# Mixer rows of x at a stride of 2304 bytes, 64 bytes behind the weight ring's residue, and all Mixer tiles over 528 columns

## The reference

```python
h = x @ w_in                    # 528 x 1024 times 1024 x 8192
b_c, c_c, h_c, q, k, v, g_conv, g_attn = split(h)
y_conv = b_c * causal_dwconv(c_c * h_c, conv_w_mix)
o = stick_breaking_attention(q, k, v)         # 16 heads of 64
merged = sigmoid(g_conv + b[0]) * (y_conv @ w_proj_conv) \
       + sigmoid(g_attn + b[1]) * (o @ w_proj_attn)
mix = merged @ w_out
# h + rms_norm(mix), then the feed-forward with its own convolution; the last 512 rows are the output
```

## Time and profile before

| what | value |
| --- | --- |
| median of 3 runs | 1918.76 us (1917.21 to 1919.23) |
| the profiled execution | 1915.86 us, of which 1914.1 us are the span |
| TensorE busy | 1900.1 us, 12180 matmuls |
| VectorE, ScalarE, GpSimd busy | 1041.9, 764.5, 66.8 us |
| the rows' DMA, mean | 88 GB/s |

### The profile page before, as it was taken

The page is one execution under the profiler, slowest core; times in us unless marked ns, Lnnn a source line. Parts: engine busy times, 40 slices in busy tenths (PEclk is TensorE's granted clock), DMA queues, the critical chain, the costliest instruction groups (busy, mean ns, idle before and its releaser), DMA issues.

```text
span 1914.1 us, 31604 instructions
## 1 busy us (share of the span) xinstructions
PE 1900.1 (99%) x12180; PEld 1694.7 (89%) x12180; DVE 1041.9 (54%) x1635; ACT 764.5 (40%) x1270; POOL 66.8 (3%) x119
## 2 busy tenths in 40 slices
PE   8999999999999999999999999999999999999998
PEld 8888888899888888888999999999999799999887
DVE  5777767445253455532646555565666464444334
ACT  5545444333233333322435554555642242333222
POOL 3000000000010000000100000000000010000000
PEclk9999999999999999999999999999999999999999
DMA  6322222232323333323232222222122233333331
GB/s 173 85 67 77 69 64 78 77 88 78 120 89 110 99 88 90 92 92 121 78 89 78 78 68 78 77 78 78 57 78 89 88 94 98 94 90 96 109 100 55
DMA packets 244260, 167.81 MB, mean 88 GB/s; under 512 B 5293, under 2 KB 231701, under 8 KB 244166
## 3 DMA queue, kind: packets, MB, share of 16 engines
q1 hardware_dynamic: 242368, 160.98, 28.4%
q10 hardware_dynamic: 1286, 4.23, 0.7%
q0 software_dynamic: 512, 1.24, 0.2%
HBM read 164.33 MB, written 2.10 MB: 87 GB/s over the span
## 4 chain that ended last, share of the span: by engine, by line
PE 92%; DVE 4%; ACT 2%; issue 1%; DMA 0%; POOL 0%; DVEq 0%; POOLq 0%; SPq 0%; ACTq 0%
PE pj L1860 9%; PE pj L1861 9%; PE pj L1862 9%; PE pj L1320 7%; PE pj L1322 7%; PE pj L1321 7%; PE zz L1320 2%; PE zz L1322 2%; PE zz L1321 2%; PE oa L1383 2%; PE tr L1383 2%; PE tr L1385 2%; PE oa L1385 2%; PE tr L1384 2%; PE oa L1384 2%; PE pj L1383 2%
## 5 line engine op out<-in xcount | busy, mean ns | idle before, releaser
L2188 DVE TENSOR_TENSOR w_lo<-raw,w_hi 128x1024 fp32r<-128x1024 f32 x299 | 364.9, 1222 | 248.4 <-ACT w_hi L681 244.6
L681 ACT ACTIVATE w_hi<-raw 128x1024 fp32r<-128x1024 f32 x299 | 314.3, 1054 | 209.5 <-PE tr L1385 140.5
L1860 PE MATMUL pj<-xx,w_hi 128*128 128x256 f32 (+2 forms) x1280 | 364.2, 285 | 0.5 <-DVE s_kl L2787 0.5
L1861 PE MATMUL pj<-xx,w_hi 128*128 128x256 f32 (+2 forms) x1280 | 360.7, 282 | 0.0
L1862 PE MATMUL pj<-xx,w_lo 128*128 128x256 f32 (+2 forms) x1280 | 360.3, 282 | 0.0
L1320 PE MATMUL pj<-xx,w_hi 128*128 128x512 f32 x632 | 252.3, 399 | 0.4 <-DVE qs L2332 0.4
L1322 PE MATMUL pj<-xx,w_lo 128*128 128x512 f32 x632 | 246.5, 390 | 0.0
L1321 PE MATMUL pj<-xx,w_hi 128*128 128x512 f32 x632 | 246.2, 390 | 0.0
L1860 PEld LDWEIGHTS pj<-xx,w_hi 128*128 128x128 f32 x1280 | 240.9, 188 | 1.9 <-issue 0.7
L1861 PEld LDWEIGHTS pj<-xx,w_hi 128*128 128x128 f32 x1280 | 241.0, 188 | 0.7
L1862 PEld LDWEIGHTS pj<-xx,w_lo 128*128 128x128 f32 x1280 | 241.1, 188 | 0.0
(11 more groups left out here) (624 smaller groups left out, 3731.8 us busy)
## 6 DMA issues: line engine op xcount, KB each, us to landing
raw<-in_l_w_in_dram SPq DMA_DIRECT2D x113, 512.0 KB, 4.1
raw<-in_w_in_dram SPq DMA_DIRECT2D x64, 512.0 KB, 4.1
raw<-in_w_up_gate_dram SPq DMA_DIRECT2D x44, 512.0 KB, 3.9
raw<-in_l_w_out_dram SPq DMA_DIRECT2D x32, 512.0 KB, 3.5
raw<-in_w_down_dram SPq DMA_DIRECT2D x22, 512.0 KB, 3.4
raw<-in_w_proj_conv_dram SPq DMA_DIRECT2D x8, 512.0 KB, 4.2
raw<-in_w_proj_attn_dram SPq DMA_DIRECT2D x8, 512.0 KB, 4.1
raw<-in_w_out_dram SPq DMA_DIRECT2D x8, 512.0 KB, 3.5
```

Of the source, the lines that this page charges most:

```text
L681: act.activation(w_hi[:, slot], raw[:, slot], ACT.Copy).then_inc(hi_done, 1)
L1860: pe.matmul(dst, w_hi[:, slot, k, :], hi[:, k, tok], start=(k == 0), stop=False)
L1861: pe.matmul(dst, w_hi[:, slot, k, :], lo[:, k, tok], start=False, stop=False)
L2188: dve.tensor_tensor(w_lo[:, slot], raw[:, slot], w_hi[:, slot].bitcast(F32), ALU.subtract).then_inc(lo_done, 1)
```

## The change

The Mixer's rows are set 576 tokens (2304 bytes) apart, beginning 64 bytes into the region of x (`XOFF` = 16 elements). Since 2304 is 9 x 256, each row then starts at the ring's residue plus 64, modulo 256. All eight tiles of a round are computed over all 528 tokens, `FULL`, 256 and 272; of q, b, c, h and the gates only the last 516 are taken from PSUM, through `P_HALF` (0 to 244 and 244 to 516 of the destination) and `P_COLS` (columns 12 to 256 of the first bank, 0 to 272 of the second). `c_hi` and `c_lo` become the first 516 elements of the same rows. The region of x grows by 3072 bytes, and the region of constants shrinks by 576: `ones_r`, `rs_hi`, `rs_lo` and `spread_rows`, which nothing called, go. To make room, small buffers of the meta tokens (`s_km`, `s_qm`, `s_zm`, `s_aTm`) move to the 48 free elements at the rows' ends, `ub`, `m_sel0` move behind the rows of the first model, `gained` of the last two junctions moves to B and `yf` to the start of A. No wait is added or removed.

```diff
@@ -155,7 +155,7 @@
...
-        const = region(4960 + 4 * P + 64 + 4 * NM)
+        const = region(4960 + 4 * NM)
@@ -165,9 +165,6 @@
...
-        ones_r = sb(const, "ones_r", [P, P], F32R)
-        rs_hi = sb(const, "rs_hi", [P, NT], F32R)
-        rs_lo = sb(const, "rs_lo", [P, NT], F32R)
@@ -203,18 +200,26 @@
...
-        X = region(2 * KD * TF * 4)
-        XA = [X[0], X[0], X[0] + 2 * KD * 576 * 4]
-        xx = sb(XA, "xx", [P, 2 * KD * 576], F32R)
+        XROW, XOFF = 576, 16
+        X = region(2 * KD * XROW * 4)
+        xx = sb([X[0], X[0], X[2] + XOFF * 4], "xx", [P, 2 * KD * XROW + XOFF], F32R)
+        X_TAIL = 2 * KD * TF * 4
...
-        x_hi, x_lo = x_view(0, TF), x_view(KD * TF, TF)
-        x3_hi, x3_lo = x_view(0, 576), x_view(KD * 576, 576)
-        X3 = 576 - T
+        x_hi, x_lo = x_view(XOFF, XROW), x_view(XOFF + KD * XROW, XROW)
+        c_hi, c_lo = x_hi[:, :, 0:TA], x_lo[:, :, 0:TA]
+        gap = sb([X[0], X[0], X[2] + XOFF * 4], "gap", [P, 2 * KD * XROW + XOFF])
+        gaps = gap[:, XOFF:XOFF + 2 * KD * XROW].rearrange("p (k t) -> p k t", k=2 * KD)
+        s_km = gaps[:, 0:KD, TF:TF + NM]
+        s_qm = gaps[:, 0:KD, TF + NM:TF + NM + MA]
+        s_zm = gaps[:, KD:KD + 2, TF:TF + NM]
+        s_aTm = gaps[:, KD + 2:KD + 6, TF:TF + 2 * NM]
+        x3_hi, x3_lo = x_view(0, XROW), x_view(KD * XROW, XROW)
+        X3 = XROW - T
@@ -222,10 +227,10 @@
...
-        def junction(q, reg, reg_gained=None):
+        def junction(q, reg):
...
-            gained[q] = sb(reg_gained or reg, f"gained{q}", [P, D])
+            gained[q] = sb(reg, f"gained{q}", [P, D])
@@ -244,8 +249,7 @@
...
-        X3_BYTES = XA[1] - X[2]
-        junction(3, again(B, KF * T * 4 + X3_BYTES - (A[2] - A[0])), again(W, (W[2] - W[0] - D * 4) // 32 * 32))
+        junction(3, again(B, KF * T * 4 - (A[2] - A[0])))
@@ -314,7 +318,7 @@
...
-        m_sel0 = sb(again(W, 227520 - 187488), "m_sel0", [GROWS, P], F32R)
+        m_sel0 = sb(again(X, X_TAIL), "m_sel0", [GROWS, P], F32R)
@@ -333,7 +337,7 @@
...
-        ub = sb(w_, "ub", [P, T])
+        ub = sb(again(X, X_TAIL + 4 * P), "ub", [P, T])
@@ -349,9 +353,6 @@
...
-        X_ = again(X)
-        c_hi = sb(X_, "c_hi", [P, KD, TA], F32R)
-        c_lo = sb(X_, "c_lo", [P, KD, TA], F32R)
@@ -362,25 +363,19 @@
...
+        assert w_[1] <= W[0] + AT_W
...
-        s_qm = sb(w_, "s_qm", [P, NP, MA])
-        s_km = sb(w_, "s_km", [P, NP, NM])
...
-        assert w_[1] <= W[0] + AT_W
-        w_ = again(W, AT_W)
...
+        s_me = sb([w_[0], w_[1], w_[2]], "s_me", [MA, HS * NM])
...
-        s_zm = sb(w_, "s_zm", [P, 2, NM])
...
-        s_aTm = sb(w_, "s_aTm", [P, P])
-        s_me = sb(w_, "s_me", [MA, HS * NM])
-        yf = sb([A[0], A[0] + X3_BYTES, B[2]], "yf", [P, KF, T])
+        yf = sb([A[0], A[0], B[2]], "yf", [P, KF, T])
@@ -394,7 +389,6 @@
...
-        assert w_[1] <= W[2] - D * 4 - 32
@@ -459,6 +453,8 @@
...
+        P_HALF = [slice(0, T // 2 - A0), slice(T // 2 - A0, TA)]
+        P_COLS = [slice(A0, T // 2), slice(0, TF - T // 2)]
@@ -1083,7 +1079,7 @@
...
-                    ins, done = act.activation(s_qh[:, par, HALF[hf]], src[:, 0:HN[hf]], ACT.Copy, scale=QD ** -0.5), "q"
+                    ins, done = act.activation(s_qh[:, par, P_HALF[hf]], src[:, P_COLS[hf]], ACT.Copy, scale=QD ** -0.5), "q"
@@ -1096,15 +1092,15 @@
...
-                    ins, done = act.activation(cb[:, HALF[hf]], src[:, 0:HN[hf]], ACT.Copy), "b"
+                    ins, done = act.activation(cb[:, P_HALF[hf]], src[:, P_COLS[hf]], ACT.Copy), "b"
...
-                    ins, done = act.activation(cx[:, KW2 - 1 + HALF[hf].start:KW2 - 1 + HALF[hf].stop], pj[:, hf, 0:HN[hf]],
+                    ins, done = act.activation(cx[:, KW2 - 1 + P_HALF[hf].start:KW2 - 1 + P_HALF[hf].stop], pj[:, hf, P_COLS[hf]],
...
-                    ins = act.activation(gates[:, g, bass.ds(p, 1), HALF[hf]], pj[:, hf:hf + 1, 0:HN[hf]], ACT.Tanh,
+                    ins = act.activation(gates[:, g, bass.ds(p, 1), P_HALF[hf]], pj[:, hf:hf + 1, P_COLS[hf]], ACT.Tanh,
@@ -1342,13 +1338,6 @@
...
-            def spread_rows(hi, lo, diag, n, done):
-                pe.wait_ge(diag, 2 * n - 1)
-                pe.matmul(rb[:, 0, :], ones_r[:], hi[:], start=True, stop=False)
-                pe.wait_ge(diag, 2 * n)
-                pe.matmul(rb[:, 0, :], ones_r[:], lo[:], start=False, stop=True).then_inc(done, 1)
@@ -1922,8 +1911,7 @@
...
-                        at, cuts = (0, FULL) if t in (1, 2) else (A0, HALF)
-                        tok = slice(at + cuts[hf].start, at + cuts[hf].stop)
+                        tok = FULL[hf]
@@ -1961,8 +1949,7 @@
...
-                        at, cuts = (0, FULL) if t in (1, 2) else (A0, HALF)
-                        halves(P_0 + t, p, 8, MX["half"], x_hi, x_lo, at, cuts, free,
+                        halves(P_0 + t, p, 8, MX["half"], x_hi, x_lo, 0, FULL, free,
@@ -2178,7 +2165,6 @@
...
-            dve.tensor_copy(ones_r[:], ones[:])
@@ -2778,8 +2764,8 @@
...
-                dve.scalar_tensor_tensor(s_ql[:, par, HALF[hf]], src[:, 0:HN[hf]], QD ** -0.5,
-                                         s_qh[:, par, HALF[hf]].bitcast(F32), ALU.mult, ALU.subtract).then_inc(MX["ql"], 1)
+                dve.scalar_tensor_tensor(s_ql[:, par, P_HALF[hf]], src[:, P_COLS[hf]], QD ** -0.5,
+                                         s_qh[:, par, P_HALF[hf]].bitcast(F32), ALU.mult, ALU.subtract).then_inc(MX["ql"], 1)
@@ -2791,7 +2777,7 @@
...
-                dve.tensor_copy(s_aTm[0:2 * NM, :], aux[0:2 * NM, 0, 512 - P:512])
+                dve.tensor_copy(s_aTm[0:2 * NM], aux[0:2 * NM, 0, 512 - P:512].rearrange("p (a b) -> p a b", a=NT))
@@ -2873,8 +2859,8 @@
...
-                            at = slice(KW2 - 1 + HALF[hf].start, KW2 - 1 + HALF[hf].stop)
-                            dve.tensor_tensor(cx[:, at], cx[:, at], pj[:, hf, 0:HN[hf]], ALU.mult).then_inc(MX["x"], 1)
+                            at = slice(KW2 - 1 + P_HALF[hf].start, KW2 - 1 + P_HALF[hf].stop)
+                            dve.tensor_tensor(cx[:, at], cx[:, at], pj[:, hf, P_COLS[hf]], ALU.mult).then_inc(MX["x"], 1)
```

## The result

The changed kernel takes 1924.37 us (median of 7, 1923.24 to 1924.52) against 1917.23 us before (median of 7), a ratio of 1.0035 with an interval of 1.0024 to 1.0045: 7.1 us slower. The profiled execution took 1924.34 us, its span is 1922.5 us. The kernel is still bound by TensorE alone.

A forecast was written before the change was run, and what follows sets the result against it. TensorE alone was taken to bound the kernel; -4.8 - 3.7 - 1.7 = -10.2 us (Mixer tiles of 516, of 528, branch) gave 1908.6 us against the median of 1918.76, range 1904 to 1926.

The forecast's parts named there:

- the rival that lets the columns cost and the place do nothing: All 64 Mixer tiles take what today's tiles of 528 take: +6.2 us, 1925.0 us; chance 0.22.
- What bounds the kernel: Whole kernel: TensorE busy 1900.1 of 1914.1 us; time is the number of matmuls times the step between starts.
- Part 1, the columns: Six of eight Mixer tiles, 48 in all, go from 516 to 528 columns: 5.76 to 6.2 us more.
- Part 2, the place of the rows: All 64 Mixer tiles, constant offset 64: 5.60 us each; -4.8 us for 48 tiles, -3.7 us for 16.
- Part 3, the branch: Eight branch tiles with c_hi and c_lo as row views, still 516 columns: 5.69 to 5.48 us each, -1.7 us.
- Parts 4 to 7: Recut evacuations, small buffers at row ends, dropped ones_r cast, shifted regions: each taken as 0, the cast at most -0.3 us.
- part 4: Evacuations of q, b, c and gates cut at 244 and 272 columns: second half under 10 ns longer, no cost.
- The reading of a collision between row stream and weight load: Mixer matmul steps: surcharge over the columns comes from a collision whose size depends on where rows and weights stand.
- The rule of the Trainium skill: TensorE matmuls: two independent read ports, surcharge about 2.5 ns whatever the addresses; sum would be near +5.8 us.
- The rival of a high lock: Mixer tiles' offset locks at the flat high step, 120 and 126.7 ns: +12.6 us, 1931.4 us; chance 0.11.

The follow-up runs named there:

- the columns-only run: Kernel before with only the 528 columns for all eight tiles, rows still 2112 bytes apart: 1923.13 us against 1917.38, ratio 1.0026.
- the map: Separate kernel, series of 24 matmuls at offsets 0 to 240 bytes between rows and weights: steps 113.3 to 120 ns for 256 columns, 123.3 to 126.7 for 272.
- the three maps: Separate series of 24 matmuls varying offset, column count, or rows and weights: for 256 columns, steps of 113.3 to 120 ns.
- the place-only run: Kernel after, with 516 columns again for six of eight tiles, moved buffers kept: 1917.72 us against 1917.38, ratio 1.0002.
- the shifted weights: Separate matmul series with weights read 64 bytes further on: 256 columns with rows at 256 bytes take 113.3 ns, against 120.0 unshifted.

## Why the prediction was right or wrong

The forecast of 1908.6 us was wrong, in sign too; the time fell on the rival that lets the columns cost and the place do nothing (1925.0), and inside the range. That it lies within 0.6 us of this rival is luck: the forecast counted from a median of three, 1918.76, and the kernel before now has 1917.23. As differences it is +7.1 against the rival's +6.2.

- **What bounds the kernel**: right. TensorE stays full, no wait came, and everything outside the two stretches kept its length.
- **Part 1, the columns**: right, 5.76 to 6.2 us foreseen, 5.75 measured alone (the columns-only run), 5.5 by the Mixer of its profile.
- **Part 2, the place of the rows**: this is the step that failed. I took 5.60 us for a tile, with 113.3 and 120 ns, from three steps at offset 112. At offset 64 the kernel's tiles take 5.87. Two errors are in it. The low steps belonged to another distance: the map has 113.3 to 114.8 at 112 for 256 columns, and of the 17 series of 256 at a distance of 64 in the three maps only one took 113.3. And 120 ns for 272 columns was made by adding the time of 16 columns to 113.3, without a row; no series of 272 goes under 123.3. The rows for the very offset, k=1 and k=5 of the earlier trace rows, gave 117 and 120 ns. I wrote that they speak against anything special at 64 and took the low step all the same; the first cut's 117.8 is what they said.
- **Part 3, the branch**: it forecast -1.7 us at the low steps. The 115 ns for 260 columns was made like the 120 for 272, by adding columns to 113.3, and no series of 260 goes under 118.3. Of the seven tiles that run through `halves`, six have steps of 117.7 to 118.1 and some 120.0, against 117.5 to 118.2 and some 119.7 before: nothing. One tile did lock low, and is the only one of its kind in the profile after: 1425.58 - 1424.22 = 1.36 us for 12 steps, 113.3 ns.

```profile
1424.22 0.28 PE L1849 MATMUL pj<-xx,w_hi 128*128 128x256 f32 x1
...
1425.58 0.28 PE L1849 MATMUL pj<-xx,w_hi 128*128 128x256 f32 x1
```


- **Parts 4 to 7**: right as far as the runs can tell; together they are in the place-only run, +0.3 us. In part 4 an evacuation was taken for an operation of 1 us; the one at cx takes 0.39 us and went from 388 ns for 260 columns to 398 for 272, which no wait shows.
- **The reading of a collision between row stream and weight load**: half of it holds. The distance from the rows to the weights decides, modulo 256 bytes, as the shifted weights show. That a constant offset would hold the low value did not follow from it: a constant offset holds a value, but which one has to be measured. That it is a collision, and of what, no run here shows: all weights of a kernel lay at one residue, so the runs don't even tell the weights that load from those in use.
- **The rule of the Trainium skill** ("TensorE: Matmul & The Clock Gate", the step-by-step section) of two independent read ports would give +5.8 us and so came nearer to the total than I did. What it says of the step does not hold here all the same: its section gives a fixed surcharge of about 2.5 ns and does not speak of addresses, and here the steps carry 6.7 to 18 ns. At equal columns one number, the offset, moved the kernel by 7 us (192 against 64), and the shifted weights moved a series of 256 columns from 120 to 113.3 ns. Whether the two ports are independent in themselves, no run here tells.
- **The rivals**: the time agrees with columns only (1925.0), but its mechanism is 1.3 us short: the place adds 7.1 - 5.75. By the steps, 64 tiles x 24 x (244.4 - 243.6) ns = 1.2 us, for 117.8 and 126.6 against the 117.8 and 125.8 of the tiles in the columns-only run; by the length of the Mixer, 452.8 - 451.3 = 1.5 us. The rival of a high lock had the right place, 126.7, for the second cut and the wrong one for the first.

What stays open is how the start of a cut picks between two values. In the version with 528 columns at 192 nearly every cut behind attention steps fell low and nearly every one directly behind a half tile high, but in the two versions with 516 columns at 192 most of both fell low, so what runs ahead of a cut does not settle it alone. In the map 2, 3 and 5 transposes ahead give different choices in two runs (at 64: 117.8, 113.3, 117.7 in one, 117.8 three times in the other), so the count of transposes is not the cause either.

## What to carry to other kernels

When TensorE is full, fp32r matmuls of some 256 columns have a price that depends on the distance, modulo 256 bytes, between the row that streams and the weights; a map of offsets and column counts costs one short run and should be made before memory is laid out anew. Look the price up for the start of each cut, for its own count of columns, and count added columns at their full time where no row shows otherwise. Means of steps are good for finding the place; what a layout brings is read from the length of the whole stage, since steps left out of a mean can take back half of it. Three low steps in a trace show that a value exists, not that a kernel will hold it, least of all at another offset.

## What the runs showed of the hardware that was not expected

- Many series settle on a multiple of 3.33 ns (8 periods of 2.4 GHz), 113.3, 116.7, 120, 123.3 or 126.7, others on a short pattern with a mean between, such as 117.8. Two values at one place exist: 113.3 and 117.8 for 256 columns at a distance of 192.
- The surcharge of a step over its columns is 6.7 to 13.3 ns for 256 columns and 10 to 13.4 for 272, and more columns can cost nothing: at 64, 272 and 280 both take 126.7 ns.
- At 512 columns the distance matters as well, 226.7 at 0, 228.9 at 64 and 231.2 at 112, but there 0 is the best of the three, where for 256 columns it is the worst.
- A single stretch of 3.4 us at the lower clock, in a kernel of 1.9 ms with a full TensorE, near 1410 or 1530 us or not at all, moves an execution by some 1.6 us, near a quarter of the 7.1 us that the change costs.
